# Who scales the softmax weights and who copies the turned tiles in block one's attention

## The reference

```
e = exp(s - max(s));  p = e / max(sum(e), tiny);  out = p @ v
```

## Time and profile before

| | us |
|---|---|
| median of three runs | 2185.71 |
| profiled execution, its own time | 2188.24 |
| span of the profiled execution | 2185.9 |
| TensorE busy | 2126.5 |
| VectorE busy | 1314.6 |
| ScalarE busy | 1178.6 |
| GpSimd busy | 0.2 |
| attention of layer 0 / layer 1 | 89.90 to 144.95 / 431.60 to 482.60 |

### The profile page before, as it was taken

The page is one execution under the profiler, slowest core; times in us unless marked ns, Lnnn a source line. Parts: engine busy times, 40 slices in busy tenths (PEclk is TensorE's granted clock), DMA queues, the critical chain, the costliest instruction groups (busy, mean ns, idle before and its releaser), DMA issues.

```text
span 2185.9 us, 33490 instructions
## 1 busy us (share of the span) xinstructions
PE 2126.5 (97%) x13434; PEld 1792.6 (82%) x13434; DVE 1314.6 (60%) x2282; ACT 1178.6 (54%) x2001; POOL 0.2 (0%) x4
## 2 busy tenths in 40 slices
PE   8999999989999999999999999999999999999998
PEld 8769999859998868887777777768888877679998
DVE  5766655766655665445665664466666336656774
ACT  5665645675544764444445343366555338447764
POOL 0000000000000000000000000000000000000000
PEclk9999999999999999999999999999999999999999
DMA  8744555754494222233122123314222323324542
GB/s 309 286 156 175 189 176 199 283 192 173 175 339 162 98 79 95 98 106 107 58 84 89 58 78 154 135 58 179 96 96 96 136 92 135 135 78 138 191 174 97
DMA packets 46968, 314.43 MB, mean 144 GB/s; under 512 B 5127, under 2 KB 7463, under 8 KB 9828
## 3 DMA queue, kind: packets, MB, share of 16 engines
q1 hardware_dynamic: 46820, 312.35, 39.5%
HBM read 311.22 MB, written 1.11 MB: 143 GB/s over the span
## 4 chain that ended last, share of the span: by engine, by line
PE 88%; ACT 5%; DVE 5%; issue 1%; DMA 0%; DVEq 0%; ACTq 0%; SPq 0%
PE bank L874 66%; PE bank L879 9%; PE bank L1287 2%; ACT ws L1427 1%; PE bank L1004 1%; DVE ws L1941 1%; PE bank L1251 1%; DVE xs L1966 1%; PE bank L1375 1%; PE bank L1354 1%; PE bank L1143 1%; DVE arena L2375 1%; PE bank L897 1%; ACT hT L1575 0%; PE bank L1172 0%
## 5 line engine op out<-in xcount | busy, mean ns | idle before, releaser
L874 PE MATMUL bank<-xs,ws 128*128 128x256 f32 (+1 forms) x9600 | 1551.7, 323 | 20.6 <-DVE xs L1966 10.6
L874 PEld LDWEIGHTS bank<-xs,ws 128*128 128x128 f32 x9600 | 1385.7, 190 | 181.0 <-DVE xs L1966 24.0
L1941 DVE TENSOR_TENSOR ws<-ring,ws 128x1024 fp32r<-128x1024 f32 x462 | 545.6, 1223 | 261.7 <-ACT ws L1427 261.2
L1427 ACT ACTIVATE ws<-ring 128x1024 fp32r<-128x1024 f32 x462 | 462.9, 1050 | 273.4 <-PE bank L874 260.2
L1966 DVE TENSOR_TENSOR xs<-arena,xs 128x512 fp32r<-128x512 f32 (+1 forms) x286 | 162.1, 582 | 277.5 <-ACT xs L1451 277.3
L1451 ACT ACTIVATE xs<-arena 128x512 fp32r<-128x512 f32 (+1 forms) x286 | 149.2, 540 | 305.6 <-PE bank L874 207.9
L879 PE MATMUL bank<-ws,xs 128*128 128x512 f32 (+1 forms) x1008 | 230.6, 388 | 4.0 <-DVE xs L1966 3.0
L1451 ACT ACTIVATE xs<-hT 128x512 fp32r<-128x512 f32 (+1 forms) x216 | 123.0, 573 | 191.1 <-PE bank L874 185.0
L879 PEld LDWEIGHTS bank<-ws,xs 128*128 128x128 f32 x1008 | 186.9, 188 | 46.1 <-DVE xs L1966 6.0
L1966 DVE TENSOR_TENSOR xs<-hT,xs 128x512 fp32r<-128x512 f32 (+1 forms) x216 | 132.8, 619 | 139.3 <-ACT xs L1451 139.1
L1963 DVE SCALAR_TENSOR_TENSOR xs<-xT,par,xs 128x256 fp32r<-128x256 f32 x112 | 51.2, 480 | 11.9 <-ACT xs L1449 11.9
(11 more groups left out here) (270 smaller groups left out, 1312.5 us busy)
## 6 DMA issues: line engine op xcount, KB each, us to landing
ring<-in_stream SPq DMA_DIRECT2D x232, 1024.0 KB, 4.8
arena<-in_side SPq DMA_DIRECT2D x57, 1024.0 KB, 7.0
arena<-gate_rows SPq DMA_DIRECT2D x8, 256.0 KB, 5.3
arena<-bias_vectors SPq DMA_DIRECT2D x1, 1536.0 KB, 9.1
hT<-in_tokens SPq DMA_DIRECT2D x1, 1024.0 KB, 5.0
arena<-in_tokens SPq DMA_DIRECT2D x1, 1024.0 KB, 12.6
out<-arena SPq DMA_DIRECT2D x2, 512.0 KB, 3.1
arena<-in_params SPq DMA_DIRECT2D x1, 918.0 KB, 8.2
```

What stands on the lines that cost most here:

```text
L874: ins = mm(ps(n, c, c + g.T), a[wi][:, p * P:(p + 1) * P], x[xi], start=first, stop=last)
L1427: do(ws[:, i % 2, 0, c], ring[:, w % R, c], ACT.Copy).then_inc(w_high, 2 // halves_in)
L1941: ins = v.tensor_tensor(ws[:, i % 2, 1, c], ring[:, w % R, c], ws[:, i % 2, 0, c].bitcast(F32), ALU.subtract)
```

## The change

GpSimd gets a program. VectorE works out the factors as before and then raises a new semaphore, `factors_ready`, in place of scaling; GpSimd waits for it and does the two scaling instructions of each of the pair's units, and raises `p_ready`. ScalarE no longer copies the transposed tile of the odd unit of a pair, except for cmp units; VectorE copies it, at the end of its own step p (behind the logits of pair p and the factors or scans of pair p-1), and so runs to step 15.

```diff
+        @block.gpsimd
+        def _(gp):
+
+            seen = Count()
+            for l in range(DEPTH):
+                for p in range(NP):
+                    if UNITS[2 * p]["kind"] == "sb":
+                        continue
+                    gp.wait_ge(factors_ready, seen(factors_ready))
+                    w, end = (16, 32) if UNITS[2 * p]["kind"] == "cmp" else (128, 384)
+                    for j in (2 * p, 2 * p + 1):
+                        s = sbuf[:, j % 6, :]
+                        nc.gpsimd.tensor_scalar(s[:, 0:w], s[:, 0:w], st[:, j, 4:5], None, ALU.mult)
+                        nc.gpsimd.tensor_scalar(s[:, w:end], s[:, w:end], st[:, j, 5:6], None, ALU.mult).then_inc(p_ready, 1)
...
                         for j in (2 * p - 4, 2 * p - 3):
                             n = N(("PT", l, j))
-                            act_.wait_ge(bank_full[n % BANKS], n // BANKS + 1)
+                            if UNITS[j]["kind"] == "cmp" or j % 2 == 0:
+                                act_.wait_ge(bank_full[n % BANKS], n // BANKS + 1)
                             if UNITS[j]["kind"] == "cmp":
                                 do(ptb[0:16, j % 4, 0:256], bank[n % BANKS][0:16, 0:256], ACT.Copy).then_inc(bank_free[n % BANKS], 1)
-                            else:
+                            elif j % 2 == 0:
                                 do(ptb[:, j % 4, :], ps(n, 0, 384), ACT.Copy).then_inc(bank_free[n % BANKS], 1)
...
-                for p in range(NP + 1):
+                for p in range(NP + 2):
                     if 0 < p < NP:
                         logits(p)
-                    if p >= 1:
+                    if 1 <= p <= NP:
...
-                            end = 32 if u["kind"] == "cmp" else 384
-                            for j in two:
-                                s = sbuf[:, j % 6, :]
-                                v.tensor_scalar(s[:, 0:w], s[:, 0:w], st[:, j, 4:5], None, ALU.mult)
-                                v.tensor_scalar(s[:, w:end], s[:, w:end], st[:, j, 5:6], None, ALU.mult).then_inc(p_ready, 1)
+                                ins = v.tensor_scalar(st2[:, :, 4:6], st2[:, :, 4:6], lam[:, 5:6], None, ALU.mult)
+                            ins.then_inc(factors_ready, 1)
+                    if 2 <= p:
+                        j = 2 * p - 3
+                        n = N(("PT", l, j))
+                        if UNITS[j]["kind"] != "cmp":
+                            dve.wait_ge(bank_full[n % BANKS], n // BANKS + 1)
+                            v.tensor_copy(ptb[:, j % 4, :], ps(n, 0, 384)).then_inc(bank_free[n % BANKS], 1)
```

More of the change, by code:

```diff
@@ L633, in build @@
         p_ready = sem("softmax_weights_ready")
+        factors_ready = sem("softmax_factors_ready")
         dfn_ready = sem("diff_normed")
@@ L2161, in _ @@
                                 dve.wait_ge(dve_own, own(dve_own))
-                            v.reciprocal(st2[:, :, 4:6], st2[:, :, 2:4]).then_inc(dve_own, 1)
-                            dve.wait_ge(dve_own, own(dve_own))
+                            ins = v.reciprocal(st2[:, :, 4:6], st2[:, :, 2:4])
                             if "gate" in u:
-                                v.tensor_tensor(st2[:, :, 4:6], st2[:, :, 4:6],
-                                                gates[:, :, u["gate"]:u["gate"] + 2].rearrange("p t u -> p u t"), ALU.mult).then_inc(dve_own, 1)
+                                ins.then_inc(dve_own, 1)
                                 dve.wait_ge(dve_own, own(dve_own))
+                                ins = v.tensor_tensor(st2[:, :, 4:6], st2[:, :, 4:6],
+                                                      gates[:, :, u["gate"]:u["gate"] + 2].rearrange("p t u -> p u t"), ALU.mult)
                             if u.get("c"):
-                                v.tensor_scalar(st2[:, :, 4:6], st2[:, :, 4:6], lam[:, 5:6], None, ALU.mult).then_inc(dve_own, 1)
+                                ins.then_inc(dve_own, 1)
                                 dve.wait_ge(dve_own, own(dve_own))
-                            end = 32 if u["kind"] == "cmp" else 384
-                            for j in two:
-                                s = sbuf[:, j % 6, :]
-                                v.tensor_scalar(s[:, 0:w], s[:, 0:w], st[:, j, 4:5], None, ALU.mult)
-                                v.tensor_scalar(s[:, w:end], s[:, w:end], st[:, j, 5:6], None, ALU.mult).then_inc(p_ready, 1)
+                                ins = v.tensor_scalar(st2[:, :, 4:6], st2[:, :, 4:6], lam[:, 5:6], None, ALU.mult)
[6 more added lines that the diff above has]
+                            v.tensor_copy(ptb[:, j % 4, :], ps(n, 0, 384)).then_inc(bank_free[n % BANKS], 1)
                     if p == 3:
```

## The result

The changed kernel takes 2218.92 us, the median of four runs (2217.76 to 2225.23), beside 2185.46 for the kernel before on the same chip (2184.75 to 2185.84): a ratio of 1.0159, 95% interval 1.0140 to 1.0179, or 33.5 us more. The direction was forecast; the size was not: 2205.3, and the time lies 1.9 us above the top of the range.

A forecast was written before the change was run, and what follows sets the result against it. It took the attention step to be bound by TensorE's order of work plus ScalarE's two copies. Copy +15.6, GpSimd's scaling 0 and clock +4 made +19.6 on 2185.7: 2205.3 us, range 2196 to 2217.

The forecast's parts named there:

- Copy on VectorE, +15.6: Both layers' attention: the copy queued late on VectorE delays TensorE's products, 6.6 us in layer 0 and 9.0 in layer 1.
- Layer 1's step 2: Attention step 2: no loss (0), because the modulation product ends last there.
- +0.53 for steps 11 and 13: Steps without modulation product: the loop through VectorE's logits, reciprocal and copy takes 3.78 us instead of 3.25.
- +0.79 for step 12: Step 12: the 0.53 us of the longer loop plus 0.26 for the lambda factor ahead of the copy.
- +1.24 for step 8: Step 8: the copy stands behind a cmp pair's factors of 1.13 us, so the product starts 1.24 us later.
- +0.05 for step 7: Step 7: short logits, a loss of about 0.05 us.
- +4.8 for steps 3 to 5: Layer 1, steps 3 to 5: the copy queued behind VectorE's scans makes step 5's product 4.8 us later.
- Steps 13 and 15: End of attention: step 15's copy queued behind the output projection's feed on VectorE, +1.1 us, including step 13's 0.53.
- So 2.0 costs nothing: GpSimd's scaling, taken as 2.0 us a pair, is hidden by 2.35 us (first unit) and about 2.8 (second).
- Rival 1: GpSimd becomes the bound at 4.4 us a pair, in some eight of ten large pairs a layer: +16, 2222; chance 0.10.
- The clock, +4: TensorE's new waits bring zero to five falls to half clock, 0 to 8 us; taken as +4, between two and three.
- The port, an estimate of 2 us: GpSimd's scaling of pairs 0 and 13 meets VectorE at the SBUF port, up to 0.4 us a meeting, both layers.

The follow-up runs named there:

- e5: Kernel before with only the odd tile's copy moved to VectorE behind factors or scans, plus zero products filling TensorE's waits: 2205.69 us, ratio 1.0092.
- e4: Changed kernel plus products of zeros filling TensorE's waits before the products of steps 3, 4, 5, 8 and 11 to 13: 2217.31 us, ratio 1.0148.
- e9: Kernel before with scaling split: VectorE scales a pair's even unit, GpSimd the odd one; ScalarE copies both tiles: 2188.58 us, ratio 1.0014.
- e2: Kernel before with VectorE copying the odd tile behind factors or scans and scaling after it; GpSimd empty: 2213.15 us, ratio 1.0125.
- e10: Changed kernel, but VectorE scales the last pair in its step 14: 2217.28 us, ratio 1.0152 to the kernel before.
- e7: Changed kernel, with TensorE issuing the next pair's logits between transposes and product: 2190.91 us, ratio 1.0024 to the kernel before.
- e1: Changed kernel, but ScalarE copies both tiles as before, leaving only GpSimd's scaling: 2204.47 us, ratio 1.0092 to the kernel before.
- e8: Kernel before with VectorE's odd-tile copy directly behind the logits and TensorE issuing next logits between transposes and product: 2188.83 us, ratio 1.0018.
- e3: Kernel before with VectorE copying the odd tile directly behind the logits, ahead of scans, factors and scaling: 2192.27 us, ratio 1.0042.
- e6: Kernel before, with TensorE issuing the next pair's logits between transposes and product: 2181.95 us, ratio 0.9987.

## Why the prediction came out as it did

| start of product to start of product, layer 1, us | 3 | 4 | 5 | 7 | 8 | 10 | 11 | 12 | 13 | 14 | 15 |
|---|---|---|---|---|---|---|---|---|---|---|---|
| before | 4.33 | 4.66 | 3.89 | 2.93 | 3.47 | 3.24 | 3.26 | 3.25 | 3.26 | 2.77 | 3.87 |
| e5 (copy alone, at full clock) | 7.20 | 5.88 | 4.70 | 2.99 | 4.70 | 3.76 | 3.79 | 4.05 | 3.78 | 2.61 | 4.87 |
| change | 7.20 | 6.90 | 5.98 | 4.66 | 4.58 | 4.66 | 3.64 | 3.91 | 5.04 | 4.93 | 3.52 |

In the last row, steps 4 and 5 and steps 13 to 15 lie for the most part at a granted 0.50.

**Copy on VectorE, +15.6: nearly right, 17.5.** e5 has the copy's place alone, with the clock held up to its last product. From the product of step 2 to that of step 15 it takes 7.2 us longer in layer 0 and 9.4 in layer 1 (forecast 6.6 and 9.0), 16.6 together. Layer 1's step 2 is 0.9 longer on top, where the prediction has 0: TensorE's product waits 0.85 us there for VectorE's copy. The single terms of layer 1 stand: +0.53 for steps 11 and 13 (measured 0.53 and 0.52), +0.79 for step 12 (0.80), +1.24 for step 8 (1.23), +0.05 for step 7 (0.06), +4.8 for steps 3 to 5 (4.90), the product of step 3 some 0.7 behind the scans. Steps 13 and 15 came to 1.5 for 1.1. Walking one step from row to row, with the releases, held to some 0.1 us in all steps but 2 and 15. By the medians e5 costs 21.3, by the traced executions 18.6 (2206.82 and 2188.24): the traced execution of the kernel before is 3.8 us above its median in that group, e5's 1.1 above its own.

**"So 2.0 costs nothing": the step that failed.** A pair takes GpSimd 2.98 us and 0.27 to start, between my 2.0 and my upper bound of 4.0. The first unit is there 1.8 us after the factors, under its 2.35 of cover, the second after 3.25, over its 2.8. The cover was wrong as well: it was worked out for a step with a full product and full logits. In step 7 the pair before is a cmp pair, whose tiles ScalarE copies, so that TensorE is through its product and 0.62 us of cmp logits and stands at the transposes at 119.09, 1.1 us after the factors: 0.50 + 0.93 us of waiting. At full clock the change less e5 gives +1.67 in step 7, +0.90 in step 10, +1.39 in steps 14 and 15 (layer 0's 3.85 and 5.02 against 2.60 and 4.88) and -0.4 in the others: 3.6 a layer, 7.2. This takes rows of one layer for both; e4 bears it out for steps 14 and 15, with 3.75 and 5.02 at full clock in either layer. Step 2, where the first pair meets TensorE early, adds 0.5 in layer 0 and 1.2 in layer 1 (2.1 less the copy's 0.9), so GpSimd costs 8.9 us. In steps 11 to 13, the only ones that I checked it in, GpSimd indeed costs nothing, since its 0.3 us waits lie beside the wait for the copy. e9 shows that it is the length. Rival 1 was this mechanism with a threshold set too high ("over 3.4 us a pair"); its place was wrong, too, as it charged eight of ten pairs alike.

**The clock, +4: too small.** Attention is 32.6 us longer; 17.5 are the copy's and 8.9 GpSimd's, worked out at full clock, so 6.2 are left for the clock. The rows give the same, each time beside the same steps at full clock. Layer 0's stretch in steps 7 and 8 costs 1.6 us (10.8 for 9.2), the one in steps 10 and 11 another 1.6 (9.9 for 8.3). In layer 1, 10.2 us at 0.50 in steps 4 and 5 cost 2.3 (12.9 for 10.6), and 10.2 us in steps 13 to 15 only 0.8 (13.5 for 12.7), since there TensorE waits for GpSimd anyway. That makes 6.3. I took between two and three slow stretches at 1.5: it was eight more than before. The price was right where one fell by itself; the two threefold ones in layer 1 are what the term lacks. I had argued from a wait of 1.35 us that was followed by no fall. In e2 the clock falls behind repeated waits of 0.45 to 1.25 us (its rows above). One wait that passed without harm says little of a loop that waits in every step, though waits of 0.73 us in every step passed without a fall too.

**The port, an estimate of 2 us: its sum about right, its single sizes not.** GpSimd's last scaling runs beside VectorE's two-input weight split in layer 0 (line 1941 of the kernel before, a part of the feed), and both are longer:

```profile
153.59 2.53 DVE L1958 TENSOR_TENSOR ws<-ring,ws 128x1024 fp32r<-128x1024 f32 x2
```

```profile
154.13 2.70 POOL L853 TENSOR_SCALAR hT<-hT,arena 128x256 f32<-128x256 f32 x1
```

The scaling takes 2.70 us for 0.92, the two splits 2.53; in e10, without GpSimd there, VectorE's two splits take 2.36. That is 1.8 us in layer 0, where the prediction had up to 0.4 a meeting; in layer 1 the same instruction took 1.19, 0.3 more. Pair 0's scaling, beside the maxima of sb, took 0.3 and 0.2 more. The places were right; that the sum, some 2.5 us, is near the 2 estimated is luck. It is a part of GpSimd's 8.9. By the Trainium skill (SBUF, "Who interferes with whom") a VectorE instruction with two inputs in SBUF contends with a GpSimd instruction that reads SBUF, and this trace agrees (2.70 us for 0.92). My estimate from the Trainium skill's rate (GPSIMD Engine Reference, 3.1 Elementwise) was 1.15 us a pair and overheads; measured are 2.98, and the measurement decides.

**The sum.** 15.6 + 0 + 4 was forecast, in a range whose own terms reach from 2199 to 2214, narrower than the 2196 to 2217 given; 17.5 + 8.9 + 6.2 = 32.6 us is measured inside attention, beside 33.5 in the medians. The three are not independent. The slow stretches of layer 0 follow GpSimd's waits in steps 7 and 10 (122.80 above: 1.12 for 0.65), those of layer 1 the copy's: e2, without GpSimd, has them at nearly the same steps (459.4 to 469.6 in steps 4 and 5, 500.4 to 507.2 in steps 13 and 14), and e5, with the copy's waits filled, has neither. Read so, about half of the clock's term, 3.2 us, goes with each, though no run takes one of them alone out of the changed kernel. That is also why e4 gains nothing: it loses the copy's 3.1 in layer 1, and the two new stretches there cost 3.1 (steps 7 and 8 take 10.8 for 9.2, steps 10 and 11 9.8 for 8.3). Outside attention the traced change is 1.7 us shorter (30.9 - 32.6), and 1.4 of it arises in one place: around 1897.7 to 1904.5 the kernel before had 6.8 us at 0.50 in block two, the change 3.4 at the same work. It does not follow the change: e5 and e7 also have 6.8 us there, e1, e2, e4, e8 and e9 3.4, and e3, e6 and e10 none.

## What to carry to other kernels

The time that an engine's work may take unseen is not one number for a loop: work it out for each kind of step, the shortest first (here the step behind a cmp pair, and the first), before calling a slower engine's work hidden. Work moved to an engine's queue costs what stands in front of it there, not its length: the same 0.55 us copy in 24 places cost 8.0 or 28.8 us by its place, and a wait in every step can cost the clock on top. Where the consumer's own next input stands behind the product that waits, try another order on TensorE as well as another engine for the copy: the order took back 27.0 of the change's 33.5 us (e7) but only 2.5 from the kernel before (e6), while who copies was worth 8.0 and 6.9 (e3; e8 beside e6).

## What the runs showed of the hardware

- GpSimd's tensor_scalar with a factor per partition, float32 in SBUF, takes 0.60 us for 128x128 and 0.92 for 128x256, where VectorE takes 0.28 and 0.35: 2.1 and 2.6 times as long.
- In e2 the granted clock of TensorE falls to 0.50 in a loop with waits of 0.45 to 1.25 us in each step; in e5, with the waits filled by products of zeros, it stays at 1.00 in the same steps. Waits of 0.73 us a step in the kernel before had no fall.
- What a stretch at 0.50 cost depended on its place in the change: 1.6 us for 3.4 us in steps 7 and 8 or 10 and 11 of layer 0, and 0.8 for 10.2 us in steps 13 to 15 of layer 1, where TensorE waits for GpSimd.
- A GpSimd tensor_scalar beside VectorE's two-input split in SBUF took 2.70 us for 0.92, and the two splits 2.53 for 2.36.
